# One fixed expert slot instead of two in a hybrid decoder step, with the second slot's gate and up weights loaded after the routing

## The reference

```
def hier_moe(h, w_rg, b_rg, w_re, b_re, w_gate, w_up, w_down):
    ...
    lg = (t @ w_rg).astype(jnp.float32) + b_rg
    pg = jax.nn.softmax(lg, axis=-1)
    g = jnp.argmax(lg, axis=-1)
    ...
    top_v, top_i = lax.top_k(le, TOP_K_IN_GROUP)
    w2 = jax.nn.softmax(top_v, axis=-1) * p_top
    ids = g[:, None] * EXPERTS_PER_GROUP + top_i
    gates = jnp.sum(jax.nn.one_hot(ids, N_EXPERTS, dtype=jnp.float32) * w2[..., None], axis=1)
    hid = jax.nn.silu(jnp.einsum('td,edf->tef', t, w_gate)) * jnp.einsum('td,edf->tef', t, w_up)
    hid = hid * gates[..., None].astype(hid.dtype)
    out = jnp.einsum('tef,efd->td', hid, w_down)
```

## Time and profile before

| | before |
|---|---|
| median of 3 runs | 929.87 us (927.68 to 932.16) |
| the profiled execution | 934.25 us, of it 932.5 us span |
| PE busy | 817.4 us (88% of the span) |
| DVE / ACT / POOL busy | 564.2 / 441.3 / 252.0 us |
| DMA moved | 154.70 MB, mean 166 GB/s |
| mean granted PE clock | 0.934 |

### The profile page before, as it was taken

The page is one execution under the profiler, slowest core; times in us unless marked ns, Lnnn a source line. Parts: engine busy times, 40 slices in busy tenths (PEclk is TensorE's granted clock), DMA queues, the critical chain, the costliest instruction groups (busy, mean ns, idle before and its releaser), DMA issues.

```text
span 932.5 us, 16339 instructions
## 1 busy us (share of the span) xinstructions
PE 817.4 (88%) x6255; PEld 508.6 (55%) x6255; DVE 564.2 (61%) x921; ACT 441.3 (47%) x855; POOL 252.0 (27%) x170
## 2 busy tenths in 40 slices
PE   3999989878999999957899999996179999998885
PEld 2766644354646644324566665553168786766652
DVE  6633569765454613168678834435756676888748
ACT  5432121568562312136466634344435667677733
POOL 2113986621332000011000000000153644544214
PEclk8999989979999999987699999999579999999998
DMA  8415886401033368853000014332696889999864
GB/s 308 96 49 166 253 267 196 158 0 46 1 96 92 120 208 260 247 207 114 0 1 1 1 46 158 136 115 91 185 340 212 275 269 298 308 329 343 243 206 193
DMA packets 98691, 154.70 MB, mean 166 GB/s; under 512 B 13573, under 2 KB 63301, under 8 KB 98610
## 3 DMA queue, kind: packets, MB, share of 16 engines
q1 hardware_dynamic: 91266, 132.97, 43.1%
q0 software_dynamic: 5728, 16.94, 7.2%
q10 hardware_dynamic: 1616, 3.70, 1.1%
HBM read 128.97 MB, written 27.48 MB: 168 GB/s over the span
## 4 chain that ended last, share of the span: by engine, by line
PE 51%; DVE 14%; ACT 9%; DMA 8%; SPq 8%; issue 7%; POOL 2%; DVEq 0%; ACTq 0%; POOLq 0%
PE ps L2238 13%; PE ps L2240 12%; PE ps L2239 12%; DMA w_reg<-in_w_up 3%; SPq L755 3%; PE ps L2577 3%; SPq L756 3%; POOL kv L890 2%; ACT w_reg L1152 1%; PE ps L2565 1%; DVE mxs L1826 1%; DVE w_reg L1498 1%; DMA gt<-q_scratch 1%; DVE mix_reg L1885 1%; PE ps L2662 1%
## 5 line engine op out<-in xcount | busy, mean ns | idle before, releaser
L890 POOL TENSOR_TENSOR kv<-kv,gt 128x1024 f32<-128x1024 f32 x32 | 80.0, 2526 | 50.9 <-DMA kv<-in_cache_k 50.8
L2238 PE MATMUL ps<-hT_reg,w_reg 128*128 128x344 f16 x288 | 89.8, 312 | 3.5 <-DVE hT_reg L1510 3.5
L2239 PE MATMUL ps<-hT_reg,w_reg 128*128 128x344 f16 x288 | 89.7, 312 | 0.0
L2240 PE MATMUL ps<-hT_reg,w_reg 128*128 128x344 f16 x288 | 89.7, 312 | 0.0
L918 POOL TENSOR_TENSOR rst<-rst,neghalf 128x1 f32<-128x1 f32 (+3 forms) x27 | 23.7, 878 | 240.5 <-DVE rst L1807 240.5
L960 POOL DMA_INDIRECT sum_scratch<-kv,dest x23 | 63.5, 2763 | 87.5 <-DMA sum_scratch<-kv,dest 82.3
L2238 PE MATMUL ps<-w_reg,hT_reg 128*128 128x512 f16 x192 | 73.5, 383 | 1.9 <-ACT kv L1141 1.9
L1264 ACT ACTIVATE hT_reg<-ps,mxn 128x128 f32<-128x128 f32 (+7 forms) x64 | 47.1, 739 | 58.1 <-DVE mxn L1827 57.5
L2239 PE MATMUL ps<-w_reg,hT_reg 128*128 128x512 f16 x192 | 73.2, 381 | 0.0
L2240 PE MATMUL ps<-w_reg,hT_reg 128*128 128x512 f16 x192 | 73.0, 380 | 0.0
L1826 DVE TENSOR_REDUCE mxs<-ps 128x1 f32<-128x640 f32 (+7 forms) x48 | 45.7, 953 | 21.1 <-PE ps L2543 11.4
(11 more groups left out here) (422 smaller groups left out, 2143.2 us busy)
## 6 DMA issues: line engine op xcount, KB each, us to landing
kv<-in_cache_k SPq DMA_DIRECT2D x64, 256.0 KB, 3.3
w_reg<-in_w_gate SPq DMA_DIRECT2D x16, 1024.0 KB
w_reg<-in_w_up SPq DMA_DIRECT2D x16, 1024.0 KB
w_reg<-in_w_down SPq DMA_DIRECT2D x16, 1024.0 KB
w_reg<-in_w_in SPq DMA_DIRECT2D x12, 1024.0 KB, 7.5
mix_reg<-in_cache_v SPq DMA_DIRECT2D x32, 256.0 KB, 3.0
kv<-in_cache_v SPq DMA_DIRECT2D x32, 256.0 KB, 3.1
mix_reg<-in_x_prompt SPq DMA_DIRECT2D x8, 512.0 KB, 8.5
```

The source lines that it names most:

```text
L890: pool.tensor_tensor(pg, pg, qbc[:, b % 2].unsqueeze(1).to_broadcast([P, 2, 512]), ALU.mult).then_inc(s_kq, 1)
L2238: pe.matmul(out, lh, rh, start=start, stop=False)
L2239: pe.matmul(out, lh, rl, start=False, stop=False)
L2240: return pe.matmul(out, ll, rh, start=False, stop=stop)
```

## The change

`FIXED` becomes 1. Expert 0 keeps slot 0 with 208 places; slots 1 to 15 are the sorted ones, with 212, 200, 188, 176, 164, 152, 140 and eight of 128 places. Against before, one slot of 208 places is gone and there is one more of 128. `FULL` becomes 2, so slot 2's list of tokens marks its empty places to be skipped, as the later slots' lists do. Since slot 1's expert is not known before the routing, SP waits for `s_re` to reach 4 ahead of `load_gate_up(1)`; the same wait further down falls away. Gate and up of slot 1 are now issued ahead of the wait for slot 0's gathered tokens, and after the order is known.

```
-FIXED = 2
+FIXED = 1
...
             sp.wait_ge(s_om, 2 * (NT + 1))
             load_down(0)
+            sp.wait_ge(s_re, 4)
             load_gate_up(1)
             sp.wait_ge(s_mlo, 2)
             sp.wait_ge(s_gx[0], y_sent(0))
-            sp.wait_ge(s_re, 4)
             load_gate_up(2)
             load_down(1)
```

## The result

The changed kernel takes 942.37 us (median of 4 runs, 938.23 to 946.50), the kernel before 928.77 us beside it (4 runs). The ratio is 1.0146, with a 95% interval of 1.0109 to 1.0184: slower by 13.6 us, 10.1 to 17.1 by the interval. The forecast was 938.9 us, from 932.5 to 944.0.

A forecast was written before the change was run, and what follows sets the result against it. Slot 0's start was bound by the gather, middle slots by PE, late slots by weight loads. Late load +13.4, slots -4.5, comparisons +0.1 make +9.0 us: 929.87 becomes 938.9 us, range 932.5 to 944.0.

The forecast's parts named there:

- The bound at the start: Start of slot 0: the gather decides it before the change; afterwards ACT's work on slot 1's late weights, queued ahead.
- The delay: ACT's reading of slot 0's tokens: moves from 679.38 to 692.8, by 13.4 us (8.7 to 14.1), weights landing at 685.5.
- My upper bound of 686.2: Latest landing of slot 1's gate and up weights beside the gathers, at 343 GB/s; a delay of 14.1 us.
- Rival B: Slot 1's load goes ahead of the gathers, landing at 680.8, delay 8.7 us; total 932.7 to 934.2 us; chance 0.16.
- The gain of the slots: Expert slots: one of 208 places goes (16.17 us), one of 128 comes (11.66 us); gain 4.5 us, 3.9 to 6.0.
- The additional slot: One more slot of 128 places, falling where the loads' lead is gone; costs one period, 11.66 us.
- The clock in slots 0 and 1: PE's half-clock stretches around slots 0 and 1: no change taken; bounds 1.9 us lost or 2.4 us given back.
- What was said to be hidden: Work behind the late load: POOL's splits, DVE's routing end and slot 2's loads cost nothing; slot 2's uncovered up to 9.2 us.
- Rival D: Late slots: the lead lost at the start stays lost, or the half clock lasts longer; 941.4 us; chance 0.17.
- Rival C: Start of slot 0: the load does not hold it up, landing by 672.1; 925.4 us; chance 0.03.
- E: Overflow part: an expert has more tokens than places, 16 passes, more than 140 us; chance 0.01.
- the comparisons: DVE's comparison of sorted experts grows from 14 x 14 to 15 x 15 elements; adds 0.1 us.

The follow-up runs named there:

- the late load alone: Kernel before, with only the wait for the order moved ahead of the load of slot 1's gate and up weights; 942.39 us, ratio 1.0143.
- reading first: Changed kernel with ACT reading slot 0's tokens before it waits for and splits slot 1's weights; 932.05 us, ratio 1.0042.
- when it was forced: Changed kernel with POOL issuing no gather before slot 1's gate and up weights have landed; 937.07 us, ratio 1.0099.
- the run with the expert given: Changed kernel with slot 1's expert written as the constant 11 and its weights loaded early, as in the kernel before; 924.77 us, ratio 0.9951.
- the expert given, loaded late: Changed kernel with slot 1's expert written as the constant 11, its load still behind the wait for the order; 939.97 us, ratio 1.0151.
- the low halves on DVE: Changed kernel with ACT reading slot 0's tokens first and DVE instead of POOL writing the low halves of slot 1's weights; 933.11 us, ratio 1.0036.

## Why the prediction was right, and which terms were mis-sized

**The bound at the start.** That ACT's order, not the gather, would decide slot 0 was right and is shown by two runs: the load alone makes the loss, and reading first takes 10.4 us of it away.

**The delay, forecast 13.4 us, measured 16.4 in the changed kernel and 13.6 with the late load alone.** The steps: the issue at 672.8, S + 1.1, was right (S + 1.06). The four activations took 7.3 us as said. The landing was forecast at 685.5, which is S + 13.8, and came at S + 16.8. Mis-sized was the rate beside the gathers. I took 365 GB/s, a rate of weight loads. From 670.0 to 685.4 the changed kernel moved 4.15 MB, 269 GB/s on average, with the DMA engines full (1.04 to 1.12 from 674 on). Table by stretches:
```profile
676.00:678.00 2.00, 0.00 (x0) 0.00 (x0) 0.00 (x0) 0.00 (x0) 0.00 (x0) 0.50 1.07 243
678.00:680.00 2.00, 0.61 (x8) 0.62 (x9) 0.00 (x0) 0.00 (x0) 0.00 (x0) 0.50 1.04 295
680.00:682.00 2.00, 0.96 (x12) 0.73 (x9) 0.59 (x1) 0.00 (x0) 0.00 (x0) 0.50 1.05 226
682.00:684.00 2.00, 0.00 (x0) 0.00 (x0) 0.00 (x0) 0.00 (x0) 0.00 (x0) 0.50 1.08 270
```
The row that I should have taken was there: gathers alone had a share of 0.90 at 262 GB/s, so a mixture could not reach 365. Of the 4.15 MB, 2.10 are slot 1's weights and 1.72 the gathers (420 rows); the other 0.33 MB are slot 2's loads, which began to run before slot 1's were through; I had them queue behind. My upper bound of 686.2, S + 14.5, was too low for the same reason. The two rows together, 1.70 MB at 262 / 0.90 = 291 GB/s and 2.10 MB at 370, would have made 11.5 us instead of 10.4, an estimate of S + 14.9; the other 1.9 us up to S + 16.8 stand in no row of before. The 13.6 us of the late load alone are no confirmation of my 13.4: there the load was issued 0.9 us earlier than I had it, and that the two numbers are so near is luck.
Rival B, the load ahead of the gathers, did not happen by itself; when it was forced, it landed at S + 9.3, where B had S + 9.1. By the Trainium skill, "DMA: Bandwidth & Descriptors", section "Queues, rings and completion order", each DMA engine takes turns between the queues; the 15.2 us beside the gathers against 7.7 alone agree with it. The same section has the descriptors of one queue taken in the order of issue on each engine, but lets a later one finish its write before an earlier one, so it does not say what slot 2's loads cost slot 1's; the 11.3 against 9.2 us do, and no run here shows how they come in between.

**The gain of the slots, forecast 4.5 us (3.9 to 6.0), measured 3.4 in the changed kernel's trace.** The period of slot 2, 16.17 us, went as said. Two terms were off.
The additional slot was dearer than 11.66. From the first gate matmul of the first slot of 128 to that of slot 15 there are 68.5 us before (six periods) and 80.6 in the changed kernel (seven), so here the slot costs 12.1 us, 0.4 more than forecast. The table by stretches has the two, before and after:
```profile
817.57:886.07 68.50, 59.66 (x757) 45.05 (x757) 56.23 (x55) 50.19 (x60) 24.76 (x12) 0.98 0.97 305
815.33:895.89 80.56, 70.82 (x881) 53.95 (x881) 66.10 (x65) 59.03 (x71) 28.21 (x14) 0.96 0.99 313
```
With the late load alone there are 69.1 us, and 80.3 to 84.8 in the nine kernels with the new order (81.7 on average), so over all traces the slot costs 11.2 to 16.3 us, 12.9 on average. I had priced it at full clock, and the clock fell in these slots. That this is what made it dearer is not shown: over the same slots the mean clock is 0.98 in three of the nine kernels, which take 80.5 to 81.2 us, and 0.96 in four, which take 80.3 to 81.9, with less idle time of PE; the DMA engines are busy for 0.98 to 1.00 in all seven. Only the two with 0.94 stand out, at 84.5 and 84.8 us and a DMA share of 0.96 and 0.95.
The period from slot 0 to slot 2 also grew, by 0.7 us in the changed kernel and by 0.4 to 0.7 in the four kernels with the new order and ACT's old order, against my "nothing". Of the 0.7, 0.5 is PE's wait for DVE's reading of slot 1's tokens, 1.73 us instead of 1.20. So the additional slot and this growth make the 1.1 us that are missing.
In the earlier trace rows the matmuls at 829.72 and 839.86 are those of slots 10 and 11, not 9 and 10. Slot 9 begins at 817.57, and its period is 12.15 us, since it also holds the down products of slot 8, which has two parts. The 10.14 us taken for the earliest slot of 128 are slot 10's; the term of 11.66 does not rest on them. The ratio of the run with the expert given, 4.5 us faster with 1.3 to 7.9, holds both 3.4 and 4.5.

**The clock in slots 0 and 1, forecast nothing, between -2.4 and +1.9.** It is within these bounds: the two periods together are 34.24 us instead of 33.55, and in this time the clock was at half up to about 699 and again after the pause between the slots, as before.

**What was said to be hidden was hidden.** POOL's split ended at 697.30, ahead of slot 1's matmuls at 711.66; the routing ended at 704.34. Rival D, a lead lost for good, is out: with the late load alone the late periods are those of before, and the loss at the end equals the delay at the start. Rival C needed a landing by S + 0.4, and E an overflow; the 16.51 MB exclude E.

**Sum.** Two errors of the same sign, 3.0 us in the delay (the rate) and 1.1 in the slots, less the 0.6 us at the end and the 0.1 us that I had added for the comparisons, make the difference between the forecast of 9.0 and the 12.4 from S on.

## What to carry to other kernels

A wait is priced by what stands behind it in the order of its engine: here 2 MB for slot 1 cost 13 to 16 us because ACT's wait for them stood ahead of the reading of slot 0's tokens, and with the order turned round, POOL's part given to DVE and the load sent behind the gather, the same change is 0.3% faster than the kernel before, at the edge of what these runs can tell. Where two transfers meet, take the rate of the slower kind for the mixture, and decide by the waits which of them goes first. A step that is moved into another engine's busy time can also block it: look at what its neighbour on POOL or DVE does in those microseconds.

## What the runs showed of the hardware that I had not expected

- An issue 0.9 us earlier brought the weights 2.7 us earlier after S (S + 14.1 in two traces against S + 16.8 to 17.0 in three). In the earlier ones the load is issued 0.1 us after POOL's first gather, in the later ones after 1.0 us. The traces also show who lands first: with the early issue slot 1's gate weights land at S + 5.5 and the first gather at S + 8.1 (the expert given, loaded late), with the later one the gate weights at S + 12.2 and the gather at S + 5.5 (tokens read first). That the early packets stand ahead of more of the gathers' fits this. But the early issues also had a constant for the expert where the later ones read a number, and the two were not separated.
- While POOL worked on 128 x 2048 elements, DVE operations of 16 and 17 elements a partition took 3.58 and 3.80 us. The Trainium skill, "SBUF — State Buffer", section "SBUF: two separate sides", says that the two engines share a pair of ports that one holds for a whole instruction while the other is blocked, where DVE's operation is in a two-port mode or has two inputs in SBUF; the trace agrees, down to the end of POOL's operations. A DVE copy of one element a partition between the two took its 0.15 us beside POOL, so not every operation is held. It goes the other way round too: with the low halves on DVE, POOL's issue of one gather took 4.53 us beside DVE's 4.47 us (about 1.0 otherwise).
```profile
692.38 4.53 POOL L948 DMA_INDIRECT hT_reg<-h_scratch,tok  x1 [17.38 <-DVE oexp L2138]
```
- In the eleven traces, of kernels that are nearly alike up to the routing, S varied by 8 us, as much as the effects that were looked for; only counting from S made the single traces comparable.
